# Weights of two k steps side by side: 1 MB transfers and a ring of six places for the experts of a one-layer recurrent decoder step

## The chip, the core and the metric

The kernel runs on one core of one Trainium2 chip. The engines named here are PE (matrix products), DVE and ACT (vector and scalar work), POOL and SP, which issue DMAs; SP here does nothing else. The metric is the device time of one execution in microseconds.

## What is computed

288 tokens (256 of a prompt, 8 sequences of 4 new ones) pass one layer: a norm, a mixer of two recurrent head groups, a second norm, then a mixture of 32 experts with four per token, an embedding term and a third norm. All is float32, and the width is 1024 throughout. Nearly all bytes are the experts' weights, three matrices of 4 MB for each of 32 experts:

```python
def _moe(x, w_router_l, b_router_l, wg, bg, wu, bu, wd, bd):
    logits = (xt @ w_router_l + b_router_l).astype(jnp.float32)
    top_v, top_i = lax.top_k(logits, TOP_K)
    gates = jax.nn.softmax(top_v, axis=-1)
    ...
        gate = xb @ wg[e] + bg[e]
        up = xb @ wu[e] + bu[e]
        gate = jnp.minimum(gate, SWIGLU_LIMIT)
        up = jnp.clip(up, -SWIGLU_LIMIT, SWIGLU_LIMIT)
        glu = gate * jax.nn.sigmoid(gate * SWIGLU_ALPHA)
        return ((up + 1.0) * glu) @ wd[e] + bd[e]
```

The layer's output adds to the normed x the experts' rows weighted by their gates, and `sigmoid(x @ w_ple_gate) * (p @ w_ple_proj)`.

## The kernel before

The kernel first runs the norm, the input projection (w_in), the recurrences, the output projection and the second norm, which writes the normed rows to `x1` (L1183 to L1191). PE transposes `x1` to `xT` (L420), and `xT` serves the router (L693) and the embedding gate (L737).

The experts are taken in pairs, 16 of them (`NPAIR`), each with a block of 64 rows per expert. In a pair there are three phases: **gate**, **up** and **down**. In each, `products` (L787) makes two bias products (L791) and then 8 k steps. A k step contracts 128 of the 1024 inputs for both experts q of the pair: the 64 gathered rows are the stationary side, the weights in the ring the moving one, in halves of 512 columns (L799). Beside the k steps PE does other work: in the gate phase it combines the pair before (`combine_unit`, L777, five units after k steps 1 to 5); in the up phase of pairs 0 to 13 it gathers rows for later pairs (`gather`, L763, after each odd k step, and a transpose of the gates at the end, L774), and in pairs 1 to 6 it makes one piece of the sample states (`sample_state`, L677).

Between up and down: DVE takes the up product in two halves (`up_half`, L1530), clamps it (L1536) and multiplies it with the gate part into `h_s` (L1538). PE transposes h (`h_transposes`, L810), four 128-column pieces for each half as soon as that half is there, ACT copies the result to `hTe`, and the down phase takes it as its stationary side. ACT copies the down product to `y_s` (L1118), which the next pair's combining units read.

**The ring** (L135) has 12 places of 128 x 1024 float32, 512 KB each. SP issues all loads in one fixed order (L296 to L306): first w_in in 2 KB rows, w_out, w_ple_gate and w_ple_proj (46 loads, `PRE`), then for each pair, matrix, k step and q one load of 4 KB rows, 48 per pair. Each waits until its place is free (`slot_free`, L275): it counts the products that last used the places (`slots_used`, or the phase's own count at the last k step). PE waits for each place by its own semaphore (L796). Input row kt * 128 + p lies in partition p, so a load reads one contiguous stretch of 512 KB.

After the pairs there may be further pairs for experts with more than 64 rows, by the same code in a loop that the data decides.

## Time and profile before

| | us |
|---|---|
| runs: median (lowest to highest) | 1408.85 (1405.63 to 1410.57) |
| the profiled execution | 1410.77 |
| its span in the profile | 1408.9 |
| PE busy | 1288.8 |
| weight loads on PE | 541.1 |
| DVE busy | 358.7 |
| ACT busy | 189.6 |
| SP's DMA queue | 430.79 MB in 121904 packets |

The profile is one execution. Its page has the busy time of each engine, then the span in 40 equal slices of 35.2 us with busy shares in tenths, the DMA engines' mean share and their rate. Views of the trace give the same for any stretch, or list instructions in order of time. A busy PE includes the ends of products that are modelled, so a phase is better measured from its first instruction to the next phase's first.

### The profile page before, as it was taken

What the parts mean: (1) busy time and instruction counts of PE and PEld (TensorE: products, weight loads), DVE (VectorE), ACT (ScalarE), POOL (GpSimd) and SP (SyncE); (2) the same over time, 40 slices, a digit from 0 to 9 for tenths busy, and PEclk for the clock granted to TensorE, in tenths of its full rate; (3) what the DMA queues carried; (4) which work ended last, traced back from release to release, by engine and by line L of the source; (5) the groups of instructions that cost most, each with busy time, mean ns of one, the idle gap of its engine ahead of it and who ended that gap; (6) DMA issues with size and microseconds to landing.
All of it is one profiled execution on the core that took longest, in us unless ns stands there. A gap on an engine that the chain in (4) does not pass through costs nothing.

```text
span 1408.9 us, 13053 instructions
## 1 busy us (share of the span) xinstructions
PE 1288.8 (91%) x5318; PEld 541.1 (38%) x5318; DVE 358.7 (25%) x528; ACT 189.6 (13%) x302; POOL 61.5 (4%) x64
## 2 busy tenths in 40 slices
PE   2899989779999999999999989999999999998984
PEld 2677678245443323233332323232333323232221
DVE  5665431334211212112121202111111211101124
ACT  3143221331110001010000101010100101010002
POOL 5000000420000000000010100000000000000000
PEclk9999975888999999999999989999999999999998
DMA  9723110121289999999999999999999999999993
GB/s 255 250 94 119 60 60 0 54 77 60 80 339 388 409 409 405 410 409 410 408 409 408 371 409 409 409 408 410 408 409 407 409 409 408 409 405 410 407 410 128
DMA packets 125614, 441.94 MB, mean 314 GB/s; under 512 B 14272, under 2 KB 14288, under 8 KB 125552
## 3 DMA queue, kind: packets, MB, share of 16 engines
q1 hardware_dynamic: 121904, 430.79, 78.4%
q0 software_dynamic: 3648, 10.27, 2.6%
q8 instruction: 45, 0.74, 0.2%
q14 instruction: 17, 0.14, 0.0%
HBM read 436.28 MB, written 4.73 MB: 313 GB/s over the span
## 4 chain that ended last, share of the span: by engine, by line
PE 76%; DMA 18%; ACT 2%; DVE 2%; issue 1%; SPq 1%; DVEq 0%
PE ps L799 38%; DMA ring<-in_w_gate 10%; PE ps L456 8%; PE ps L767 7%; PE ps L783 6%; DMA ring<-in_w_up 4%; PE ps L644 3%; PE ps L743 3%; DMA ring<-in_w_in 2%; DMA ring<-in_w_down 2%; PE ps L791 1%; PE ps L484 1%; ACT hTe L935 1%; PE ps L597 1%; PE ps L815 1%
## 5 line engine op out<-in xcount | busy, mean ns | idle before, releaser
L799 PE MATMUL ps<-ring,xTe 128*64 128x512 f32 x2048 | 482.6, 601 | 17.0 <-DMA ring<-in_w_up 8.4
L799 PEld LDWEIGHTS ps<-ring,xTe 128*64 128x64 f32 x2048 | 134.2, 136 | 316.6 <-issue 315.6
L799 PE MATMUL ps<-ring,hTe 128*64 128x512 f32 x1024 | 236.8, 612 | 16.8 <-DMA ring<-in_w_down 16.8
L1520 DVE TENSOR_TENSOR xs<-xs,ps 128x512 f32<-128x512 f32 (+1 forms) x96 | 65.7, 685 | 501.8 <-PE ps L783 501.6
L799 PEld LDWEIGHTS ps<-ring,hTe 128*64 128x64 f32 x1024 | 73.4, 140 | 173.0 <-issue 172.8
L456 PE MATMUL ps<-xT,ring 128*128 128x288 f32 x448 | 118.1, 422 | 6.3 <-DMA ring<-in_w_in 5.3
L767 PE MATMUL ps<-OH,x 128*128 128x256 f32 (+3 forms) x432 | 115.4, 389 | 0.0
L456 PEld LDWEIGHTS ps<-xT,ring 128*128 128x128 f32 x448 | 86.8, 197 | 32.7 <-DMA ring<-in_w_in 6.4
L767 PEld LDWEIGHTS ps<-OH,x 128*128 128x128 f32 (+1 forms) x432 | 67.3, 187 | 72.9 <-issue 66.5
L783 PE MATMUL ps<-y_s,GT 128*128 128x512 f32 (+1 forms) x192 | 88.2, 630 | 1.1 <-ACT y_s L935 1.1
L1536 DVE TENSOR_SCALAR h_s<-ps 128x512 f32<-128x512 f32 x32 | 22.0, 687 | 188.0 <-PE ps L799 188.0
L935 ACT ACTIVATE xTe<-ps 128x256 f32<-128x256 f32 (+1 forms) x60 | 23.9, 398 | 298.0 <-PE ps L767 298.0
L935 ACT ACTIVATE h_s<-g_s 128x1024 f32<-128x1024 f32 x16 | 16.9, 1057 | 324.6 <-DVE g_s L1526 324.6
L935 ACT ACTIVATE y_s<-ps 128x1024 f32<-128x1024 f32 x16 | 16.4, 1024 | 265.1 <-PE ps L799 265.1
L644 PE MATMUL ps<-ring,xT 128*128 128x512 f32 (+1 forms) x96 | 39.7, 635 | 8.8 <-DVE xT L1438 8.8
L783 PEld LDWEIGHTS ps<-y_s,GT 128*128 128x128 f32 (+1 forms) x192 | 21.4, 161 | 65.4 <-issue 61.3
L791 PE MATMUL ps<-bias,sel 96*128 96x512 bf16 x96 | 29.0, 384 | 13.3 <-ACT hTe L935 13.0
L743 PE MATMUL ps<-ring,xT 128*128 128x512 f32 (+1 forms) x96 | 38.5, 621 | 0.0
L935 ACT ACT_TABLE_LOAD x28 | 35.9, 1283 | 14.6 <-DVE mv L1181 12.2
L380 POOL TENSOR_TENSOR T<-V,cf 32x1024 f32<-32x1024 f32 x8 | 16.3, 2044 | 414.1 <-PE ps L686 348.7
L1526 DVE TENSOR_SCALAR g_s<-ps 128x1024 f32<-128x1024 f32 x16 | 19.6, 1225 | 33.9 <-PE ps L799 33.9
L644 PEld LDWEIGHTS ps<-ring,xT 128*128 128x128 f32 (+1 forms) x96 | 13.7, 174 | 32.5 <-issue 23.5
(304 smaller groups left out, 732.5 us busy)
## 6 DMA issues: line engine op xcount, KB each, us to landing
ring<-in_w_gate SPq DMA_DIRECT2D x256, 512.0 KB, 11.7
ring<-in_w_up SPq DMA_DIRECT2D x256, 512.0 KB, 11.4
ring<-in_w_down SPq DMA_DIRECT2D x256, 512.0 KB, 11.4
ring<-in_w_in SPq DMA_DIRECT2D x28, 512.0 KB, 5.7
ring<-in_w_out SPq DMA_DIRECT2D x8, 512.0 KB, 4.2
ring<-in_w_ple_gate SPq DMA_DIRECT2D x8, 512.0 KB, 3.7
S<-in_state_hgrn_S POOLq DMA_DIRECT2D x1, 2048.0 KB, 20.3
out<-S POOLq DMA_DIRECT2D x1, 2048.0 KB, 20.8
```

The lines of the kernel that those rows point to most:

```text
L380: nc.gpsimd.tensor_tensor(VB[n % len(VB)][0:NS, :].rearrange("p (b v) -> p b v", b=NSEQ), V[0:NS, 2, off:off + DV].unsqueeze(1).to_broadca ...
L456: last = mm(ps[:, bank, 0:NT], w, xT[:, k, :], start=k == 0, stop=k == KT - 1)
L644: last = mm(out_banks(i, half), HT[:, k, t0:t0 + r], w[:, half * 512:(half + 1) * 512], start=k == 0, stop=k == KT - 1)
L743: last = mm(ple_bank(i, half, bank), xT[:, k, t0:t0 + r], ring[:, n % RING, half * 512:(half + 1) * 512], start=k == 0, stop=k == KT - 1)
L767: last = mm(ps[:, bank, (k - k0) * w:(k - k0 + 1) * w], x1[0:r, i, k * P:(k + 1) * P], OH[0:r, i, c0:c0 + w], start=i == 0, stop=i == 2)
L783: last = mm(ps[lo:lo + r, CB_BANKS[n], :], gt[:, t0:t0 + r], y_s[:, half * 512:(half + 1) * 512], start=True, stop=True)
L791: mm(ps[:, bank0 + half, :], sel_p[:, :, :].rearrange("p q s -> p (q s)"), bias3[:, w, half * 512:(half + 1) * 512], start=True, stop=False)
L799: last = mm(ps[64 * q:64 * q + 64, bank0 + half, :], lhs(k, q), ring[:, s, half * 512:(half + 1) * 512], start=False, stop=k == KT - 1)
L935: return nc.scalar.activation(out, in_, func, **kw)
L1520: last = tt(x, x, ps[lo:lo + r, CB_BANKS[n], :], ALU.add)
L1526: ts(g_s[:, :], ps[:, 0:2, :].rearrange("p b n -> p (b n)"), LIMIT, None, ALU.min).then_inc(S["gl_ok"], 1)
L1536: ts(h_s[:, c], ps[:, 2 + half, :], LIMIT, -LIMIT, ALU.min, ALU.max).then_inc(S["u_ok"], 1)
```

## The change

Two things are regrouped. **Which input row lies in which partition**: not kt * 128 + p but p * 8 + kt, so that a partition owns eight consecutive input rows of a weight, and two consecutive k steps are 8 KB side by side in memory. **How the ring is used** by the experts: six places of 1 MB (`NWIDE`), 24 loads per pair (`PER = 3 * KT`), each with k steps 2 kw and 2 kw + 1 for one expert. A load's 128 rows then lie 32 KB apart. w_in, w_out and the embedding's weights keep loads of 512 KB; w_ple_gate and w_router only take the new row order.

Since contraction index k step kt, partition p now means input 8 p + kt, the other side of each product has to be in that order too. This is done where x1 and h are written, by DVE: `x1` and h get their columns reordered through `by_row`. h goes to `y_s` instead of `h_s`, each half of it fills 64 columns of each of the eight pieces, and so both halves have to be there before the first transpose. The transposes' own code stays.

```diff
-PER = 6 * KT
+NWIDE, PRE_WIDE = RING // 2, PRE // 2
+PER = 3 * KT
...
-    w_pg = a["w_ple_gate"][0].rearrange("(kt p) n -> kt p n", p=P)
+    w_pg = a["w_ple_gate"][0].rearrange("(p kt) n -> kt p n", p=P)
...
-    w_ex = [a[n].rearrange("l e (kt p) n -> (l e) kt p n", p=P) for n in ("w_gate", "w_up", "w_down")]
+    w_ex = [a[n].rearrange("l e (p kw k2) n -> (l e) kw p (k2 n)", p=P, k2=2) for n in ("w_gate", "w_up", "w_down")]
...
+        def wide(d):
+
+            return ring[:, 2 * (d % NWIDE):2 * (d % NWIDE) + 2, :]
...
+        def by_row(t):
+
+            return t.rearrange("r (k p) -> r p k", k=KT)
...
+            def wide_free(d, j=None):
+
+
+                if d - NWIDE < PRE_WIDE:
+                    return sp.wait_ge(S["slots_used"], 2 * (d - NWIDE) + 2)
+                p, t = divmod(d - NWIDE - PRE_WIDE, PER)
+                w, n = divmod(t, KT)
+                if n >= KT - 2:
+                    sem, count, per = S[("gate_mm", "up_mm", "y_mm")[w]], 4 * (p + 1), 4
                 else:
+                    sem, count, per = S["slots_used"], PRE + p * USED_PER + w * (KT - 2) + n + 1, USED_PER
+                sp.wait_ge(sem, count if j is None else j * per + count)
...
             for p in range(NPAIR):
-                for w in range(3):
-                    for k in range(KT):
-                        for q in range(2):
-                            ring_load(w_ex[w][2 * p + q, k], False)
+                for t, (w, k, q) in enumerate((w, k, q) for w in range(3) for k in range(KT // 2) for q in range(2)):
+                    d = PRE_WIDE + p * PER + t
+                    wide_free(d)
+                    sp.dma_start(wide(d).rearrange("p k n -> p (k n)"), w_ex[w][2 * p + q, k]
+                                 ).then_inc(slot_full[2 * (d % NWIDE)], 16)
...
                 for k in range(KT):
-                    slots = [(PRE + first + 2 * k + q) % RING for q in range(2)]
-                    for q, s in enumerate(slots):
-                        pe.wait_ge(slot_full[s], p * (16 * PER // RING) + 16 * ((PRE + first + 2 * k + q) // RING + 1))
+                    tiles = [first + 2 * (k // 2) + q for q in range(2)]
+                    if k % 2 == 0:
+                        for t in tiles:
+                            pe.wait_ge(slot_full[2 * ((PRE_WIDE + t) % NWIDE)], p * (16 * PER // NWIDE) + wide_full(t))
...
                             if k == KT - 1:
                                 last.then_inc(done, 1)
-                            elif half == 1:
+                            elif half == 1 and k % 2 == 1:
                                 last.then_inc(S["slots_used"], 1)
...
-                pe.wait_ge(S["h_ok"], p * 2 + (half + 1))
+                pe.wait_ge(S["h_ok"], p * 2 + 2)
...
-                    last = nc.tensor.transpose(ps[:, bank, j * P:(j + 1) * P], h_s[:, c:c + P], ident)
+                    last = nc.tensor.transpose(ps[:, bank, j * P:(j + 1) * P], y_s[:, c:c + P], ident)
...
-                out = x1[0:r, i, :] if 4 <= n < 7 else x
-                stt(out, x, mv[0:r, i, 3:4], ln_b[0:r, :], ALU.mult, ALU.add).then_inc(S["x_norm"], 1)
+                if 4 <= n < 7:
+                    last = stt(by_row(x1[0:r, i, :]), x.rearrange("r (p k) -> r p k", k=KT), mv[0:r, i, 3:4],
+                               ln_b[0:r, :].rearrange("r (p k) -> r p k", k=KT), ALU.mult, ALU.add)
...
-                    stt(h_s[:, c], h_s[:, c], 1.0, g_s[:, c], ALU.add, ALU.mult).then_inc(S["h_ok"], 1)
+                    stt(by_row(y_s[:, :])[:, 64 * half:64 * half + 64, :], h_s[:, c].rearrange("r (p k) -> r p k", k=KT), 1.0,
+                        g_s[:, c].rearrange("r (p k) -> r p k", k=KT), ALU.add, ALU.mult).then_inc(S["h_ok"], 1)
...
-                step(ts(xs[0:r, i, :], x1[0:r, i, :], ALPHA, None, ALU.mult))
+                step(ts(xs[0:r, i, :].rearrange("r (p k) -> r p k", k=KT), by_row(x1[0:r, i, :]), ALPHA, None, ALU.mult))
```

The queue of SP's loads over the gate and up phases of one pair, before; a row is one or several issues of a form, with the semaphore that frees the place (`y_mm` and `gate_mm` count the last k step of a phase):

```order
L293 DMA ring<-in_w_gate 128x1024 [waits slots_used] x10
L293 DMA ring<-in_w_gate 128x1024 [waits y_mm] x2
L293 DMA ring<-in_w_gate 128x1024 [waits slots_used] x4
L293 DMA ring<-in_w_up 128x1024 [waits slots_used] x10
L293 DMA ring<-in_w_up 128x1024 [waits gate_mm] x2
L293 DMA ring<-in_w_up 128x1024 [waits slots_used] x4
```

And with the change:

```order
L320 DMA ring<-in_w_gate 128x2048 [waits slots_used] x4
L320 DMA ring<-in_w_gate 128x2048 [waits y_mm] x2
L320 DMA ring<-in_w_gate 128x2048 [waits slots_used] x2
L320 DMA ring<-in_w_up 128x2048 [waits slots_used] x4
L320 DMA ring<-in_w_up 128x2048 [waits gate_mm] x2
L320 DMA ring<-in_w_up 128x2048 [waits slots_used] x2
```

There are half as many issues, each of 2048 columns, in the same order of matrices.

PE between the up and the down phase of pair 0, before (`cf` holds the identity for the transposes, `slot_full` a place's semaphore):

```order
L815 MATMUL ps<-cf,h_s 128x128 [waits h_ok]
L815 MATMUL ps<-cf,h_s 128x128 x3
L815 MATMUL ps<-cf,h_s 128x128 [waits h_ok]
L815 MATMUL ps<-cf,h_s 128x128 x3
L791 MATMUL ps<-bias_112,sel_113 128x512 [waits hTe_ok,GT_ok]
L791 MATMUL ps<-bias_112,sel_113 128x512
L799 MATMUL ps<-ring,hTe 64x512 [waits slot_full7,slot_full6]
L799 MATMUL ps<-ring,hTe 64x512 x3
L799 MATMUL ps<-ring,hTe 64x512 [waits slot_full9,slot_full8]
```

And with the change:

```order
L831 MATMUL ps<-cf,y_s 128x128 [waits h_ok]
L831 MATMUL ps<-cf,y_s 128x128 x3
L831 MATMUL ps<-cf,y_s 128x128 [waits h_ok]
L831 MATMUL ps<-cf,y_s 128x128 x3
L806 MATMUL ps<-bias_112,sel_113 128x512 [waits hTe_ok,GT_ok]
L806 MATMUL ps<-bias_112,sel_113 128x512
L815 MATMUL ps<-ring,hTe 64x512 [waits slot_full8,slot_full6]
L815 MATMUL ps<-ring,hTe 64x512 x7
L815 MATMUL ps<-ring,hTe 64x512 [waits slot_full0,slot_full10]
```

No instruction changes places. A pair of places is now waited for once for eight products instead of four, and both waits for `h_ok` ask for the second half.

## Rows read from the trace of the kernel before

**Rows 1.** The page: the DMA engines' rate in 40 slices.

```profile
GB/s 255 250 94 119 60 60 0 54 77 60 80 339 388 409 409 405 410 409 410 408 409 408 371 409 409 409 408 410 408 409 407 409 409 408 409 405 410 407 410 128
```

**Rows 2.** A window: length, busy PE, PEld, DVE, ACT, POOL, PE's clock, DMA share, GB/s.

```profile
600.00:800.00 200.00, 196.07 (x812) 65.69 (x809) 38.60 (x51) 16.11 (x29) 13.85 (x13) 1.00 1.03 408
```

**Rows 3.** The page's chain that ended last, by engine.

```profile
PE 76%; DMA 18%; ACT 2%; DVE 2%; issue 1%; SPq 1%; DVEq 0%
```

**Rows 4.** Timeline of PE: first products of pairs 0, 1, 2, 6, 7, 14, 15.

```profile
384.29 0.59 PE L791 MATMUL ps<-bias,sel 96*128 96x512 bf16 x2 [0.35 <-PE ps L757]
...
447.31 0.61 PE L791 MATMUL ps<-bias,sel 96*128 96x512 bf16 x2
...
508.24 0.61 PE L791 MATMUL ps<-bias,sel 96*128 96x512 bf16 x2
...
511.47 1.94 PE L799 MATMUL ps<-ring,xTe 128*64 128x512 f32 x8 [0.62 <-DMA ring<-in_w_gate]
...
755.22 0.60 PE L791 MATMUL ps<-bias,sel 96*128 96x512 bf16 x2
...
830.98 0.60 PE L791 MATMUL ps<-bias,sel 96*128 96x512 bf16 x2
...
1263.48 0.60 PE L791 MATMUL ps<-bias,sel 96*128 96x512 bf16 x2
...
1324.85 0.61 PE L791 MATMUL ps<-bias,sel 96*128 96x512 bf16 x2
```

**Rows 5.** Timeline of PE inside pairs 3 and 4.

```profile
617.84 13.95 PE L799 MATMUL ps<-ring,hTe 128*64 128x512 f32 x64
...
636.40 1.13 PE L783 MATMUL ps<-y_s,GT 128*128 128x512 f32 x2
...
665.91 1.98 PE L686 MATMUL ps<-T,AB 32*128 32x512 f32 x4
...
677.18 1.09 PE L815 MATMUL ps<-cf,h_s 128*128 128x128 f32 x8
```

**Rows 6.** PE's waits in pairs 7 to 13: total us, times, longest.

```profile
PE ps L799 <- DMA ring<-in_w_down: 7.8, 14, 0.6
PE ps L799 <- DMA ring<-in_w_gate: 4.3, 7, 0.6
```

**Rows 7.** The page: packets of SP's queue, and issues with median us to landing.

```profile
q1 hardware_dynamic: 121904, 430.79, 78.4%
...
ring<-in_w_ple_gate SPq DMA_DIRECT2D x8, 512.0 KB, 3.7
```

**Rows 8.** A window in which w_in is loaded.

```profile
44.00:48.00 4.00, 4.00 (x18) 3.16 (x17) 3.86 (x5) 0.41 (x1) 0.00 (x0) 1.00 1.05 388
```

**Rows 9.** Timeline of DVE, the end of pair 4's up phase.

```profile
676.36 0.69 DVE L1538 SCALAR_TENSOR_TENSOR h_s<-h_s,g_s 128x512 f32<-128x512 f32 x1
```

**Rows 10.** DVE by line and form: busy us, mean ns of one, idle before.

```profile
L1299 DVE TENSOR_TENSOR T<-KB,T 128x576 f32<-128x576 f32 x5 | 3.8, 753 | 3.3 <-PE ps L500 3.3
...
L1190 DVE SCALAR_TENSOR_TENSOR x<-xs,mv,ln_b 128x1024 f32<-128x1024 f32 x2 | 2.6, 1284 | 2.7 <-ACT mv L935 2.7
...
L1483 DVE TENSOR_REDUCE pick<-oneh 128x32 f32<-128x128 f32 x2 | 0.7, 372 | 0.1
...
L1481 DVE TENSOR_TENSOR oneh<-cf,top_f 128x128 f32<-128x128 f32 x2 | 0.6, 292 | 0.1
```

**Rows 11.** Timeline of PE, between up and down in pair 14.

```profile
1305.23 0.66 PE L815 MATMUL ps<-cf,h_s 128*128 128x128 f32 x4 [0.73 <-DVE h_s L1538]
```

**Rows 12.** Two links of the chain of waits after the second norm.

```profile
308.69 1.29 DVE x L1190
...
320.62 0.63 PE ps L430 x4
```

**Rows 13.** Timeline of DVE after the second norm, and ahead of the experts.

```profile
318.51 1.27 DVE L1190 SCALAR_TENSOR_TENSOR x<-xs,mv,ln_b 32x1024 f32<-32x1024 f32 x1 [0.64 <-ACT mv L935]
...
377.05 0.69 DVE L1546 TENSOR_TENSOR ple<-ple,ps 128x512 f32<-128x512 f32 x1 [21.41 <-PE ps L757]
```

More of the change, by code:

```diff
@@ L223, in trunk_step, with wide_full @@
         ps = ctx.enter_context(nc.psum_tensor("ps", [P, 8, 512], F32))
+        def wide(d):
+            return ring[:, 2 * (d % NWIDE):2 * (d % NWIDE) + 2, :]
+        def wide_full(t):
+            s = (PRE_WIDE + t) % NWIDE
+            return 16 * (len(range(2 * s, PRE, RING)) + len(range(s, PRE_WIDE + t + 1, NWIDE)) - len(range(s, PRE_WIDE, NWIDE)))
+        def by_row(t):
+            return t.rearrange("r (k p) -> r p k", k=KT)
         ident = cf[:, CF_IDENT:CF_IDENT + P]
@@ L302, in _ @@
             for p in range(NPAIR):
[L303 to L306 removed]
+                for t, (w, k, q) in enumerate((w, k, q) for w in range(3) for k in range(KT // 2) for q in range(2)):
[3 more added lines that the diff above has]
+                                 ).then_inc(slot_full[2 * (d % NWIDE)], 16)
             def extra_weights(j, e):
[L310 to L313 removed]
+                for t, (w, k, q) in enumerate((w, k, q) for w in range(3) for k in range(KT // 2) for q in range(2)):
+                    d = PRE_WIDE + NPAIR * PER + t
+                    wide_free(d, j)
+                    sp.dma_start(wide(d).rearrange("p k n -> p (k n)"),
                                  w_ex[w][bass.ds(e[q], 1), k, :, :].rearrange("e p n -> p (e n)")
[L315 removed]
+                                 ).then_inc(slot_full[2 * (d % NWIDE)], 16)
             sp.wait_ge(S["pos_ok"], 1)
@@ L793, in products @@
                 for k in range(KT):
-                    slots = [(PRE + first + 2 * k + q) % RING for q in range(2)]
-                    for q, s in enumerate(slots):
-                        pe.wait_ge(slot_full[s], p * (16 * PER // RING) + 16 * ((PRE + first + 2 * k + q) // RING + 1))
+                    tiles = [first + 2 * (k // 2) + q for q in range(2)]
+                    if k % 2 == 0:
+                        for t in tiles:
+                            pe.wait_ge(slot_full[2 * ((PRE_WIDE + t) % NWIDE)], p * (16 * PER // NWIDE) + wide_full(t))
                     for half in range(2):
-                        for q, s in enumerate(slots):
+                        for q, t in enumerate(tiles):
                             last = mm(ps[64 * q:64 * q + 64, bank0 + half, :], lhs(k, q),
-                                      ring[:, s, half * 512:(half + 1) * 512], start=False, stop=k == KT - 1)
+                                      wide(PRE_WIDE + t)[:, k % 2, half * 512:(half + 1) * 512], start=False, stop=k == KT - 1)
                             if k == KT - 1:
                                 last.then_inc(done, 1)
-                            elif half == 1:
+                            elif half == 1 and k % 2 == 1:
                                 last.then_inc(S["slots_used"], 1)
@@ L888, in _ @@
                 products(p, 0, 0, lhs, 0, sel[p % 2], lambda k: beside_gate(p, k), S["gate_mm"])
-                products(p, 2 * KT, 2, lhs, 1, sel[p % 2], lambda k: beside_up(p, k), S["up_mm"])
+                products(p, KT, 2, lhs, 1, sel[p % 2], lambda k: beside_up(p, k), S["up_mm"])
                 for half in range(2):
@@ L894, in _ @@
                 pe.wait_ge(S["hTe_ok"], 2 * p + 2)
-                products(p, 4 * KT, 4, lambda k, q: hTe[:, k, 64 * q:64 * q + 64], 2, sel[p % 2],
+                products(p, 2 * KT, 4, lambda k, q: hTe[:, k, 64 * q:64 * q + 64], 2, sel[p % 2],
                          nothing, S["y_mm"])
@@ L916, in _ @@
                         products(p, 0, 0, x_cols(xTe[0], 0), 0, sel[0], nothing, S["gate_mm"])
-                        products(p, 2 * KT, 2, x_cols(xTe[0], 0), 1, sel[0], nothing, S["up_mm"])
+                        products(p, KT, 2, x_cols(xTe[0], 0), 1, sel[0], nothing, S["up_mm"])
                         for half in range(2):
@@ L920, in _ @@
                         pe.wait_ge(S["hTe_ok"], j * 2 + (2 * NPAIR + 2))
-                        products(p, 4 * KT, 4, lambda k, q: hTe[:, k, 64 * q:64 * q + 64], 2, sel[0], nothing, S["y_mm"])
+                        products(p, 2 * KT, 4, lambda k, q: hTe[:, k, 64 * q:64 * q + 64], 2, sel[0], nothing, S["y_mm"])
                         pe.wait_ge(S["GT_ok"], j + (NPAIR + 1))
```

21 lines of the change are left out of this document (5 added, 16 removed).

## The prediction, made before the changed kernel ran

> **What bounds the kernel now.** I read the slices first. From slice 14 to slice 39 the rate stands at 405 to 410 GB/s with one dip [rows 1]: this is the expert stage, which moves 16 pairs x 24 MB = 403 MB. A window in it shows a DMA share of 1.03 and PE busy 196 of 200 us at full clock [rows 2]. So both are near their end at once, and the chain (PE 76%, DMA 18% [rows 3]) can't tell which gives way. For that I cut the stage into pairs of experts, by the first bias product of each gate phase [rows 4]. Numbering the pairs 0 to 15: pair 1 takes 508.24 - 447.31 = 60.9 us, with no wait for a DMA; pairs 1 to 5 take 61.6 on average; pair 6 takes 75.8 (the sample states are written out then); pairs 7 to 13 take (1263.48 - 830.98) / 7 = 61.8; pair 14 takes 61.4. The DMA's need for 24 MB at 408 GB/s is 61.7. PE's own need is 60.9 where it also makes a sample state (pairs 1 to 6), and 2.0 less, 58.9, in pairs 7 to 13, since the state's products cost 1.98 [rows 5]. There it waits for weights in short pieces, most in down and gate phases [rows 6]. So **pairs 1 to 6 are bound by PE and DMA almost alike, pairs 7 to 15 by the DMA**. Pair 0 takes 63 us of PE's work.
>
> **Part 1: the size of a piece of a transfer.** The DMA engines show 121,904 packets on SP's queue [rows 7]. Counting rows of the loads and outputs in the code gives 108,736, plus 16 per issue for 823 issues = 13,168: exactly that sum. So each row in a partition is one packet (the constants' rows of 4,384 bytes too), and I take an 8 KB row to be one. What is a packet's fixed cost? w_in comes in 2 KB rows and ran at 388 GB/s with a full share [rows 8]; the experts' 4 KB rows run at 408 to 409 [rows 2]. Per engine and 32 KB: 32,768 B / (388/16) = 1351 ns, and 1282 ns at 409. The 8 packets fewer save 69 ns, 8.7 ns each. Going to 8 KB saves 4 more, and half a semaphore packet: 1282 - 39 = 1243 ns, or 421 GB/s. **A 1 MB transfer then takes 2.49 us, a pair 59.8 us**, 2.0 less than the 61.8 of pairs 7 to 13. Bounds: no gain at all (2.57 us), or nothing left of the cost (about 1.5% more still).
> The Trainium skill ("DMA: Bandwidth & Descriptors", Why small descriptors are slow) gives about 3 cycles per packet beside one per 32 bytes. By it 128 + 3 becomes 256 + 3, a gain of 1.1% and not 3%, and the sum below would end near +13 us rather than +6. The row at 388 speaks for the larger cost.
>
> **Part 2: the ring.** Six places of 1 MB hold what twelve of 512 KB held, but a place comes free only after two k steps, and PE needs two places whole to start. What is the price? Where PE is slower than the DMA (the up phase, with gathers), the ring is full at the start of a down phase, D. PE does 8 k steps in 13.95 us [rows 5], so it frees two places at D + 4.0, 7.5, 10.9 and 14.4. A transfer of 512 KB on an idle queue landed 3.7 us after its issue [rows 7], 2.4 more than its 1.28 on the engines (the experts' own landing times are time in the queue). So the down phase's fourth piece (k 6 and 7) lands at 4.0 + 2.4 + 5.0 = 11.4, where PE wants it at 10.9: wait 0.4. The next two land 5.0 apart, at 16.4 and 21.3. PE wants them at 14.4 + 0.4 + 0.5 = 15.4 (wait 1.0) and at 16.4 + 3.5 + 1.2 = 21.0, with a combining unit (1.13 and the switch) between [rows 5] (wait 0.3). Then units of 1.2 after each k step make PE slower than the DMA again. **Total 1.7 us per pair.** Before, with a full ring and single places, the same sum gives no wait: pair 1 has none.
>
> **Part 3: h is written scattered.** Each half of h now goes to y_s with neighbours 512 bytes apart, and both halves are needed before the first transpose. Where gathers run, the second half's product ends at 676.36 + 0.69 = 677.05 [rows 9] and the transposes start at 677.18, when PE gets there [rows 5]: the lost overlap costs nothing there. But any lengthening d of the two products shows, less 0.13. ACT's copies and PE's down phase stand behind it. In pairs 14 and 15 PE already waits for h [rows 11], but there the DMA is the bound and catches it. No write of this kind is in the trace. Nearest row: a reduction that reads elements 128 bytes apart takes 372 ns for 128 elements, where a product of 128 takes 292 [rows 10]: 80 more, so 0.34 us per 512 written elements. d = 0.68, less 0.13 = 0.55 per pair. Bounds: 0, and a doubling of what an element costs, i.e. the same operation's 1,024-element form less its 512 one (1.28 - 0.69 = 0.59 each) [rows 10], 1.05 per pair. I take 0.55, the only row with far-apart elements.
> The Trainium skill ("SBUF — State Buffer", Door 1) says that each access crossing to a new 16-byte line pays a penalty. It speaks against this change, and gives no figure; by it the case of no cost is out.
>
> **The sum**, stage by stage, for d' = 0.55:
> Pairs 1 to 6: 60.9 + 1.7 + d' against 61.6: +1.6 each, +9.6 (pair 6 keeps its stall).
> Pairs 7 to 13: 58.9 + 1.7 + d' = 61.2 (more than the DMA's 59.8) against 61.8: -0.6 each, -4.0.
> Pair 14: the DMA's 59.8 against 61.4: -1.6. Pair 15: -1.6, but after the last byte two k steps remain and not one, +1.7: 0.
> Pair 0: 0.4 + d' = +1.0.
> Expert stage: +5.0.
> Ahead of it: x1 is written scattered three times after the second norm. The first is in the chain (1.29 us [rows 12]), the third ends at 318.51 + 1.27 = 319.78 [rows 13], 0.8 before its transposes start. With 0.67 more on each, the third ends at 321.8 and PE starts about 1.2 later than 320.62; 0 or 2.7 at the bounds. The scaling of x1 into xs lies in an idle stretch of DVE (21.4 us before L1546 [rows 13]), and its longer time is hidden. w_ple_gate and w_router are loaded long before use.
> Total +6.2: the profiled execution goes from 1410.8 (span 1408.9) to 1417.0. The median of the runs shown, 1408.85, is 1.9 below the profiled one, so **1415.1**.
>
> **Rivals.**
> A. Scattered writes are free. For: products that read and write runs of 1 to 16 elements with gaps as long stay at 753 ns for 576 [rows 10], like packed ones. Against: the gaps there are short. Sum: 5.0 - 14 x 0.55 = -2.7, nothing ahead: 1406.1.
> B. An element costs double. Sum: 5.0 + 14 x 0.50 + 2.7 = +14.7: 1423.6. It decides from d' = 1.1 us or so, where pairs 7 to 13 too become no shorter than they were (58.9 + 1.7 + d' = 61.8).
> C. 8 KB rows bring no rate (cut in two, or the pitch of 32 KB between a partition's rows costs what the length gives). Transfer 2.57: waits 2.2, pairs 1 to 6 +2.1 each, 7 to 13 none, 14 none, 15 +1.7, pair 0 +1.2, front +1.2: +17, 1425.5. This is also the case in which the change doesn't do what it says.
> D. The refill waits don't arise, since transfers land sooner after a place is free than I have it. Then pairs 7 to 13 fall to the DMA's 59.8 (-14), pairs 1 to 6 keep still (-0.6), 14 and 15 -1.5, pair 0 and front +1.7: -14.4, 1394.5. Against: pair 2 already waits in its gate phase although pair 1 had none to wait for [rows 4], so lead times under load are not shorter than I take them.
>
> **Chances.** Forecast 0.34, A 0.27, B 0.19, C 0.10, D 0.10. A measurement can tell about 0.3%, 4.2 us, from no change. Each case has some 4 us to either side from the lead time of a transfer. Faster: D 0.10, A 0.13, forecast 0.04 = 0.27. Same: A 0.12, forecast 0.10, B 0.01 = 0.23. Slower: C 0.10, B 0.18, forecast 0.20, A 0.02 = 0.50. The range takes in A, B, most of C and the nearer half of D: 1397 to 1426. The forecast's own range is 1410 to 1421.
>
> **What would show it.** Packets on SP's queue down by 49,152 + 6,144, and 421 GB/s in windows without idle DMA. DVE's h product at 1.03 us (0.69 for A, 1.28 for B). Pairs 1 to 6 at 63.2, pairs 7 to 13 at 61.2, pair 14 at 59.8. DMA share below 1 in the up phases, as the ring is full. PE waiting for gate weights in pieces of about 1 us at k 0, and at k 2, never between. I am wrong if the DMA share stays at 1.03 through pairs 7 to 13, or if the rate is not near 420.

## The result, and the profile after

| | before | after | forecast |
|---|---|---|---|
| median of the runs | 1408.99 us (6 runs, 1405.63 to 1410.57) | 1429.27 us (6 runs, 1428.57 to 1437.48) | 1415.1 |
| profiled execution: time, span | 1410.8, 1408.9 | 1429.0, 1427.2 | 1417.0 |
| pairs 1 to 5, mean | 61.6 | 63.8 | 63.2 |
| pairs 6 and 7 | 75.8, 61.9 | 70.9, 66.3 | 77.4, 61.2 |
| pairs 8 to 13, mean | 61.8 | 61.8 | 61.2 |
| pair 14; pair 15 and the end | 61.4; 84.1 | 63.3; 87.7 | 59.8; 84.1 |

The change made the kernel slower: ratio 1.0157, 95% interval 1.0132 to 1.0182. I had forecast slower, but by 6 us and not by 20; the time lies 3 us outside the range. (Periods of pairs are cut as in [rows 4]: from one gate phase's bias product to the next.)

The page of the changed kernel, its DMA rate in 40 slices and SP's queue, which answer to [rows 1, 7]:

```profile
GB/s 255 247 90 118 59 59 0 62 68 59 109 344 390 418 379 378 422 378 422 360 421 379 410 400 408 379 397 423 400 422 397 411 407 397 422 397 422 381 399 94
...
q1 hardware_dynamic: 66608, 430.77, 75.0%
```

The packets fell by 121,904 - 66,608 = 55,296, exactly the 49,152 + 6,144 foreseen, and where the queue is never empty the rate is 422 GB/s. But the slices no longer stand at one level: those at 422 alternate with ones at 360 to 400. Windows of the changed kernel (length, busy PE, PEld, DVE, ACT, POOL, PE's clock, DMA share, GB/s), first the one of [rows 2], then pair 9: its gate phase, and the turn from up to down:

```profile
600.00:800.00 200.00, 190.79 (x786) 64.93 (x782) 38.12 (x48) 16.25 (x29) 7.51 (x4) 0.99 0.96 395
971.00:975.00 4.00, 3.73 (x16) 1.13 (x14) 0.69 (x1) 0.00 (x0) 0.00 (x0) 1.00 1.01 424
...
1015.00:1018.00 3.00, 3.00 (x16) 1.01 (x14) 0.00 (x0) 0.00 (x0) 0.00 (x0) 1.00 0.85 352
1018.00:1021.00 3.00, 3.00 (x16) 1.01 (x14) 0.00 (x0) 0.00 (x0) 0.00 (x0) 1.00 0.71 229
1021.00:1024.00 3.00, 3.00 (x16) 1.00 (x14) 0.00 (x0) 0.00 (x0) 0.00 (x0) 1.00 1.01 418
```

A faster DMA moved less: 395 GB/s over 600:800, where it was 408. It pauses for a while in each pair, while PE is busy. The timeline of PE at that pause (start, us, engine, line, operation, records, idle before it and its releaser) tells why:

```profile
1005.43 3.65 PE L815 MATMUL ps<-ring,xTe 128*64 128x512 f32 x16
1009.01 1.75 PE L782 MATMUL ps<-OH,x 128*128 128x256 f32 x6
1010.70 0.61 PE L789 MATMUL ps<-cf,GW 128*128 128x128 f32 x3
1011.79 1.09 PE L831 MATMUL ps<-cf,y_s 128*128 128x128 f32 x8 [0.48 <-DVE y_s L1558]
1013.71 0.59 PE L806 MATMUL ps<-bias,sel 96*128 96x512 bf16 x2 [0.83 <-ACT hTe L951]
1014.23 10.52 PE L815 MATMUL ps<-ring,hTe 128*64 128x512 f32 x48
1025.93 3.65 PE L815 MATMUL ps<-ring,hTe 128*64 128x512 f32 x16 [1.18 <-DMA ring<-in_w_down]
...
1030.90 3.65 PE L815 MATMUL ps<-ring,xTe 128*64 128x512 f32 x16 [0.78 <-DMA ring<-in_w_gate]
```

Up's last k step ends at 1009.0 and gives back two places. The next two come back when down's second k step is over, at 14.2 + 3.6 = 1017.9. For 8.9 us nothing is freed; the ring fills up, and the DMA stands. PE pays for it at the end of the down phase (1.18) and at the next gate (0.78). Before, a place was half as large and came back after one k step, and the share stayed at 1.01 to 1.03 there.

### The profile page after: what moved, and what is told of

Read it like the earlier page. It is cut to its first block, busy times and chain, and to the rows that moved or that the text cites. A ratio compares the mean times of both kernels' runs of the same rounds, so it can differ in the third digit from the quotient of the medians.

```text
span 1427.2 us, 12477 instructions
## 1 busy us (share of the span) xinstructions
PE 1285.9 (90%) x5318; PEld 551.2 (39%) x5318; DVE 369.8 (26%) x528; ACT 189.5 (13%) x302; POOL 61.1 (4%) x64
## 3 DMA queue, kind: packets, MB, share of 16 engines
q1 hardware_dynamic: 66608, 430.77, 75.0%
## 4 chain that ended last, share of the span: by engine, by line
PE 69%; DMA 21%; DVE 6%; ACT 2%; issue 1%; SPq 1%; DVEq 0%
PE ps L815 36%; DMA ring<-in_w_gate 11%; PE ps L471 8%; PE ps L782 6%; DMA ring<-in_w_up 6%; PE ps L798 4%; PE ps L758 3%; PE ps L659 3%; DMA ring<-in_w_in 2%; DVE y_s L1558 2%; DMA ring<-in_w_down 2%; DVE h_s L1556 1%; PE ps L499 1%; PE ps L806 1%; ACT hTe L951 1%
## 5 line engine op out<-in xcount | busy, mean ns | idle before, releaser
L815 PE MATMUL ps<-ring,xTe 128*64 128x512 f32 x2048 | 477.5, 601 | 29.8 <-DMA ring<-in_w_gate 19.4
L815 PEld LDWEIGHTS ps<-ring,xTe 128*64 128x64 f32 x2048 | 140.6, 137 | 320.1 <-issue 319.8
L815 PE MATMUL ps<-ring,hTe 128*64 128x512 f32 x1024 | 234.2, 610 | 14.4 <-DMA ring<-in_w_down 14.4
L798 PEld LDWEIGHTS ps<-y_s,GT 128*128 128x128 f32 (+1 forms) x192 | 21.4, 161 | 65.4 <-issue 61.3
L1558 DVE SCALAR_TENSOR_TENSOR y_s<-h_s,g_s 128x512 f32<-128x512 f32 x32 | 33.4, 1043 | 1.1
L831 PE MATMUL ps<-cf,y_s 128*128 128x128 f32 x128 | 19.2, 298 | 12.0 <-DVE y_s L1558 12.0
## 6 DMA issues: line engine op xcount, KB each, us to landing
S<-in_state_hgrn_S POOLq DMA_DIRECT2D x1, 2048.0 KB, 20.3
```

The source lines that it names most:

```text
L798: last = mm(ps[lo:lo + r, CB_BANKS[n], :], gt[:, t0:t0 + r], y_s[:, half * 512:(half + 1) * 512], start=True, stop=True)
L815: last = mm(ps[64 * q:64 * q + 64, bank0 + half, :], lhs(k, q), wide(PRE_WIDE + t)[:, k % 2, half * 512:(half + 1) * 512], start=False, st ...
L831: last = nc.tensor.transpose(ps[:, bank, j * P:(j + 1) * P], y_s[:, c:c + P], ident)
L1558: stt(by_row(y_s[:, :])[:, 64 * half:64 * half + 64, :], h_s[:, c].rearrange("r (p k) -> r p k", k=KT), 1.0, g_s[:, c].rearrange("r (p k) ...
```

## The experiments

All ratios are to the kernel before, which ran beside them at 1408.75 to 1409.44 us. Four parts can be told apart: the row order with scattered writes, the size of the places, the 8 KB rows, and what PE does.

### The parts alone

**e_fine**: the kernel before (twelve places of 512 KB, 4 KB rows) with the row order and the scattered writes.

```diff
-    w_ex = [a[n].rearrange("l e (kt p) n -> (l e) kt p n", p=P) ...
+    w_ex = [a[n].rearrange("l e (p kt) n -> (l e) kt p n", p=P) ...
```

> The row order of the change alone (partition p owns input rows 8p to 8p+7, h and x1 written scattered, both halves of h awaited), but loads of one k step, 4 KB rows, 512 KB, in the old ring of twelve places. If the coarse ring is what costs (my theory now: places of 1 MB come free late and are refilled late), this kernel stands near the one before: rate 408 to 409, pairs 1 to 6 at 61.8, pairs 7 to 13 at 61.8, plus 0.9 ahead of the experts and 1 to 2 at pairs 14 and 15: 1411 to 1414. If the new row order costs (rows 32 KB apart, the scattered writes), it stands near the changed kernel: 1425 to 1430, and the first of the two shows as a rate below 405.

Measured 1420.24 us (1.0088, 1.0065 to 1.011), at 407 GB/s over 905:1263, for 408 before: the pitch of 32 KB between rows costs the DMA nothing that shows, but the row order costs 11 us with a fine ring, more than I gave it.

**e_wide4k**: six places of 1 MB and transfers of 1 MB, but in the old order, so in 4 KB rows, with plain writes.

```diff
-    w_ex = [a[n].rearrange("l e (p kw k2) n -> (l e) kw p (k2 n)", p=P, k2=2) ...
+    w_ex = [a[n].rearrange("l e (kw k2 p) n -> (l e) kw p k2 n", p=P, k2=2) ...
```

> The coarse ring alone: six places of 1 MB, transfers of 1 MB, but the old row order, so each partition gets two rows of 4 KB, and h and x1 are written plainly and awaited by halves as before. Coarse ring theory: rate 409, pairs 1 to 6 at 60.9 + 2.5 = 63.4, pairs 7 to 13 at 61.7 to 62, the last two about 1.5 longer than before: 1420 to 1426. Row order theory: as before, 1407 to 1411.

Measured 1429.88 us (1.0157, 1.0138 to 1.0175). **The coarse ring alone costs 21 us**, as much as the whole change. A window in pairs 8 to 13, of this kernel, then the same one of the kernel before, shows PE busy 4.6 us less in the same time:

```profile
905.00:1263.00 358.00, 337.57 (x1409) 116.16 (x1405) 60.66 (x84) 28.78 (x50) 0.00 (x0) 1.00 1.02 405
```

```profile
905.00:1263.00 358.00, 342.13 (x1430) 114.98 (x1428) 59.90 (x83) 29.66 (x53) 0.00 (x0) 1.00 1.03 408
```

In pairs 1 to 5 a pair takes 64.4 us for 61.6; that is 14 of the 19 us between the two spans. Three things are coarse here at once: the places, the transfers that fill them, and the 2 MB that come back together. No run changes one of them alone.

**e_plain**: the changed kernel with h, x1 and the scaled x1 written plainly. Both halves of h are still awaited together. The weights' rows then meet other elements of x1 and h, so the experts' and the embedding gate's part of the result is not the reference's.

```diff
-                    stt(by_row(y_s[:, :])[:, 64 * half:64 * half + 64, :], h_s[:, c].rearrange("r (p k) -> r p k", k=KT), 1.0, ...
+                    stt(y_s[:, c], h_s[:, c], 1.0, g_s[:, c], ALU.add, ALU.mult)
```

> The changed kernel with h, x1 and the scaling of x1 written and read plainly (the contraction then pairs the wrong rows, so the experts' part of the output is not the reference's; the work is the same). Expected, if the scattered writes cost what DVE's 1.04 us and PE's waits of 0.48 show: 0.48 less in pairs 0 to 13, 1 to 2 less in 14 and 15, 0.9 less ahead: 1417 to 1420. If DVE's time were covered: no change from 1429. If it carries the whole loss: 1409.

Measured 1415.32 us (1.0047, 1.003 to 1.0063). So the writes cost 14.0 of the change's 20.3 us. And beside e_wide4k, which has the same ring, **the 8 KB rows give back 14.6 us**, and a little more, since e_wide4k may start on the first half of h alone: in each of pairs 14 and 15 it waits 1.4 us for h, and e_plain 2.06.

**e_pestride**: the changed kernel with h written plainly, and PE's transposes reading every eighth column of it; x1 as in the change.

```diff
-                    last = nc.tensor.transpose(ps[:, bank, j * P:(j + 1) * P], y_s[:, c:c + P], ident)
+                    last = nc.tensor.transpose(ps[:, bank, j * P:(j + 1) * P], h_s[:, 4 * half + j:D:KT], ident)
```

> The changed kernel, but h is written plainly and PE's transposes read every eighth column of it instead. If a strided read is free on PE: as e_plain plus 0.9 for x1, 1418 to 1421. If PE reads strided elements at a lower pace (transposes at 2 times 0.14 us each per pair), up to 1.1 us per pair more: 1433.

Measured 1419.14 us (1.0073, 1.0054 to 1.0093): the scattered h is 10.1 of the 14.0 us, x1 the other 3.8. The runs' intervals leave some 3 to 4 us to either side of each such difference. The step is not quite free for PE either: in pairs 0 to 13 the eight transposes take 1.16 us for 1.09. Their weight loads, in e_pestride and then in the changed kernel (window 390:1290):

```profile
L830 PEld LDWEIGHTS ps<-cf,h_s 128*128 128x128 f32 x112 | 13.6, 194 | 0.6
```

```profile
L831 PEld LDWEIGHTS ps<-cf,y_s 128*128 128x128 f32 x112 | 12.0, 141 | 8.3 <-DVE y_s L1558 8.3
```

### The ring

**e_before8** and **e_after8**: one line, `RING = 12` to `RING = 8`, in the kernel before and in the changed one: 4 MB instead of 6.

> The kernel before with eight 512 KB places instead of twelve (4 MB). 3 MB are left to run ahead of the step in use. Theory of the coarse ring: between the change's 4 MB (1429 less its other parts) and four wide places' 2 MB: 1425 to 1460, and well under e_after8. Rival, depth hardly matters: 1409 to 1415.

> The changed kernel with four 1 MB places instead of six (4 MB), nothing else. Theory of the coarse ring: only 2 MB, some 5 us of transfer, can run ahead of the place in use, less than the gathers and the hand-over of h hold the TensorE and about the time from a freed place to its landed refill (3.1 us) plus the other place; each pair loses 4 to 8 us: 1480 to 1560. Rival, depth hardly matters and the writes do: 1429 to 1440.

Measured 1459.17 us (1.0357, 1.0325 to 1.0388) and 1645.78 us (1.1658, 1.1606 to 1.1709), the second 86 us over the upper end of what I expected. With 4 MB in fine places the kernel loses 50 us, and in coarse ones 217 over the change. I read depth and grain as one thing, how much of the ring is not in use. PE holds one 1 MB step of it before, and 2 MB after, so 5, 4, 3 and 2 MB are left in the kernel before, e_wide4k, e_before8 and e_after8, which take 1409, 1430, 1459 and 1646 us (the last also has the scattered writes and 8 KB rows). PE's waits in e_after8 (total us, times, longest):

```profile
PE ps L815 <- DMA ring<-in_w_down: 73.8, 19, 6.3
PE ps L815 <- DMA ring<-in_w_gate: 63.1, 40, 3.5
PE ps L815 <- DMA ring<-in_w_up: 54.0, 37, 3.8
```

**e_qfirst** and **e_qfirst_pe**: can coarse places come back one by one? The block of expert q=0 on both k steps goes ahead of that of q=1; the second kernel also writes all plainly and has PE read x1 and h with a step.

```diff
+                    if k < KT - 2:
+                        steps = [(kk, half, k % 2) for kk in (k - k % 2, k - k % 2 + 1) for half in range(2)]
...
+                    for kk, half, q in steps:
+                        last = mm(ps[64 * q:64 * q + 64, bank0 + half, :], lhs(kk, q), ...
```

> The changed kernel, with the four matmuls of expert q=0 on both k steps of a 1 MB place issued ahead of the four of q=1 (k steps 0 to 5; 6 and 7 as they are). The same matmuls, as many between two gathers or combine units; only each expert's tile is waited for when its own block comes, and its place is given back a block (about 0.85 us) earlier. Theory of the coarse ring (two places of 1 MB given back together leave 4 of 6 MB to run ahead; the old kernel's places left 5): a ring whose places come back one by one leaves 5 MB again, so 1412 to 1419 us against the change's 1429.3, the pair's waits on DMA at gate k2 and up k2/k4/k6 gone. Rival, the scattered writes or the matmul side are what costs: 1426 to 1430, the waits as they were.

> The same, with h, x1 and the scaled x1 written plainly and every reordering left to TensorE, which reads x1 and h with a step of 8 columns (as it did for h without a visible cost). Theory of the coarse ring, with the row order's DVE cost (1.0 us per h, 1.3 us per x1 tile) taken away: the 8 KB rate is left alone, so 1396 to 1405 us, under the old kernel's 1409. Rival, the row order costs through something other than the writes: 1412 or more.

Measured 1642.1 us (1.1658, 1.1639 to 1.1678) and 1667.1 us (1.1825, 1.1805 to 1.1845), so this said nothing about the ring, but much about PE. The timeline of e_qfirst, where x8 is four matmuls:

```profile
1114.00 3.65 PE L818 MATMUL ps<-ring,xTe 128*64 128x512 f32 x8
```

Four matmuls take 3.65 us, the time of eight in the changed kernel (x16 above). The two experts' products go to rows 0 to 63 and 64 to 127 of the result, and two of them run at once only while q alternates. The Trainium skill says in "TensorEngine Tiling (Array Packing)", Key Properties, that tiles operate independently and can run in parallel; this trace agrees.

### PE beside the DMA

**e_half_before** and **e_half_after**: each expert product on 256 columns instead of 512, in both kernels; the other columns of the products hold the bias only.

```diff
-                            last = mm(ps[64 * q:64 * q + 64, bank0 + half, :], lhs(k, q), ...
+                            last = mm(ps[64 * q:64 * q + 64, bank0 + half, 0:256], lhs(k, q), ...
```

> The kernel before with its expert products on half the columns (each matmul 256 instead of 512; the other half of h and y holds only the bias), all transfers as they are. It leaves TensorE some 38 us of a 61 us pair, so the pairs run at the rate of the weights alone: 61.4 us (24 MB at 409 GB/s). Theory of two bounds (TensorE is busy 60.5 us in pairs 1 to 6 and 58.5 in 7 to 13, and must wait 1.3 us more for the hand-over of h, so it has as little room as the DMA): only the gaps of pairs 1 to 6 and the end of pair 15 go: 1380 to 1400 us. Rival, TensorE had room and the DMA alone is the bound: 1390 to 1405, which tells little by itself; the two runs are read together.

> The changed kernel with the same halved products. Theory of two bounds: with TensorE out of the way the 8 KB rows show their whole worth, 59.8 us per pair instead of 61.4: 20 to 25 us under e_half_before, the pairs at 59.8 +- 0.4, since neither the coarse ring nor the DVE's writes can hold back a TensorE with 20 us to spare. Rival, the coarse ring or the row order holds back the DMA queue whatever TensorE does: within 8 us of e_half_before.

Measured 1404.13 us (0.9964, 0.9953 to 0.9974) and 1393.3 us (0.988, 0.9862 to 0.9898): 11 us between them, half of the 20 to 25. (e_half_before lies 4 us over my theory's 1380 to 1400, within its rival's range.) Windows of e_half_after tell where the rest is:

```profile
536.00:540.00 4.00, 4.00 (x8) 1.26 (x10) 0.45 (x1) 0.00 (x0) 0.41 (x1) 0.50 1.01 422
540.00:544.00 4.00, 4.00 (x14) 2.08 (x10) 0.77 (x1) 0.00 (x0) 1.48 (x1) 0.50 0.78 279
...
905.00:1263.00 358.00, 265.74 (x1461) 139.43 (x1460) 63.84 (x85) 30.68 (x54) 0.00 (x0) 0.89 1.01 420
```

From 905 on it does keep to 420 GB/s. The first two windows are of pair 2's up phase: PE, which had waited 2.49 and 1.76 us for weights, runs at a granted clock of 0.50 (1.2 of 2.4 GHz), is slow just where it has most to do, and the DMA's share falls to 0.78. I take it that the coarse ring is full there. e_half_before's PE waits too (its clock is 0.87 on average in pairs 1 to 6, for 0.84), but with its fine ring the share is 1.03 over these pairs and 1.02 over 905:1263.

**e_thin_before** and **e_thin_after**: the gathers for later pairs make one matmul of 32 rows instead of three (the prompt's rows are left out of them).

```diff
                     for i, (_, r) in enumerate(TILES):
+                        if w == 128 or i == 2:
...
-                                  OH[0:r, i, c0:c0 + w], start=i == 0, stop=i == 2)
+                                      OH[0:r, i, c0:c0 + w], start=w > 128 or i == 0, stop=i == 2)
```

> The kernel before with the gathers for later pairs cut from three matmuls to the one of 32 rows (the rows of the two prompt tiles are left out of xTe), all signals and transfers as they are. It takes 1.1 us from each of four gathers, 4.5 us of TensorE time from each pair of 0 to 13, with its clock kept high. Theory of two bounds: the DMA's 61.4 us per pair stays, so 1400 to 1408 us. Rival, TensorE alone is the bound of this kernel: 4 us less per pair, 1350 to 1370.

> The changed kernel with the same thin gathers. Theory of two bounds and a coarse ring: without those 4.5 us TensorE's path is 57 us in pairs 1 to 6 and 55 in 7 to 13, under the DMA's 59.8, and the time between two freed pairs of places shrinks too: 1390 to 1402 us, 27 to 40 less than the change and under e_thin_before by 3 to 15, the pairs at 59.8 to 61. Rival, the landing time of a refill holds it whatever TensorE does: 1412 or more, over e_thin_before.

Measured 1406.66 us (0.9984, 0.9973 to 0.9995), as expected: the kernel before keeps the DMA at 408 GB/s and has PE at its heels. And 1439.45 us (1.0204, 1.0179 to 1.023): **with some 60 us less to do for PE (14 pairs, four gathers each at 0.69 us and not 1.75) the changed kernel is 10 us slower**. The rival's "1412 or more" holds, but neither theory had it slower than the change. Its windows at the turn from up to down in pair 9:

```profile
1020.00:1022.00 2.00, 2.00 (x6) 0.55 (x8) 0.00 (x0) 0.00 (x0) 0.00 (x0) 0.50 1.01 422
1022.00:1024.00 2.00, 2.00 (x10) 0.62 (x8) 0.00 (x0) 0.00 (x0) 0.00 (x0) 0.69 1.01 422
1024.00:1026.00 2.00, 2.00 (x12) 0.58 (x10) 0.00 (x0) 0.00 (x0) 0.00 (x0) 1.00 0.17 66
1026.00:1028.00 2.00, 2.00 (x12) 0.68 (x10) 0.00 (x0) 0.00 (x0) 0.00 (x0) 1.00 0.63 131
```

Three things come together. The gather that stood between up's last k step and the transposes had covered the DVE's two products of h; with it thin, PE waits for h (26.5 us in all instead of 12.0). PE's waits for weights grow more, from 44 to 73 us. After such a wait the clock is 0.50, so down's first k steps take longer. And the stretch without a freed place grows with both, so the DMA stands longer (share 0.17, then 0.63). No run splits the 10 us among them.

**e_mg_before**, **e_mg_after**: the four gathers moved from up's k steps 1, 3, 5, 7 to down's 0, 2, 4, 6, to even out the phases. **e_mg2_before**, **e_mg2_after**: only two of them moved, to down's k steps 1 and 3, behind a freed place.

```diff
+            def beside_down(p, k):
+                if p < GATHERS and k % 2 == 0:          # e_mg2: k in (1, 3)
...
+                    gather(xTe[g % 2], 4 * (p % 2) + n, 1, 6 + n % 2, 0, 256)
```

> The kernel before with its four gathers for the next pairs moved from behind up's k steps 1, 3, 5, 7 to behind down's 0, 2, 4, 6 (and ACT's and DVE's copies behind those of h), nothing else. Gate, up and down then take TensorE 20, 19 and 21 us instead of 20, 26 and 14, while the weights of each take the DMA 20.5. Theory: the ring of 5 free MB already carries the uneven phases over, so it gives little: 1402 to 1412. Rival, uneven phases cost the kernel before too: 1395 or less.

> The changed kernel with the same move. Theory of the coarse ring (its 4 free MB run full during the long up phase, the DMA pauses, and TensorE starves at the start of down and of gate): with even phases the ring never runs full, and most of the change's 20 us come back: 1403 to 1415. Rival, it is the landing time of a 1 MB refill and not the uneven phases: 1420 to 1430.

> The kernel before with only the third and fourth gather moved: up keeps two, behind its k steps 1 and 3, and down takes two, behind its k steps 1 and 3. Gate, up and down take TensorE 20, 23 and 18 us. Theory: as e_mg_before, little to gain with fine places: 1403 to 1413 us. Rival, even phases help by themselves: under 1400.

> The changed kernel with the same move. In e_mg_after the gathers stood behind even k steps, between the two k steps of one place, and put 1.75 us more ahead of the first place that down frees; the ring then stood full for some 8 us of each down phase. Here they stand behind odd k steps, after a place was freed. Theory of the gap between freed places (what costs is the stretch in which TensorE frees nothing and the six places run full): the gap at up to down is that of the change and the long up phase is shorter: 1410 to 1425. Rival, any work moved into down costs the changed kernel as in e_mg_after: 1450 to 1495.

Measured 1413.87 us (1.0025, 1.0014 to 1.0036) and 1415.06 us (1.0042, 1.0028 to 1.0057) for the old kernel, 1495.78 us (1.0622, 1.0599 to 1.0646) and 1447.26 us (1.0271, 1.0248 to 1.0293) for the changed one. The old kernel's are 2 us over what I expected; of the changed one's, the first is 66 us over even its rival's range and the second 3 us under its rival's. Evening out the phases gained nothing; what is moved into down makes the kernel slower. A gather between down's first two k steps adds 1.75 us to it, and those taken from up's end had covered the wait for h (the line below, for 12.0 us in the changed kernel). Windows of e_mg_after, one in gate and two in down, and PE's wait for h in e_mg2_after:

```profile
1018.00:1022.00 4.00, 4.00 (x18) 1.02 (x14) 0.95 (x2) 0.00 (x0) 0.00 (x0) 1.00 0.99 342
...
1054.00:1058.00 4.00, 4.00 (x16) 1.53 (x14) 0.00 (x0) 0.38 (x1) 0.00 (x0) 0.83 0.38 154
1058.00:1062.00 4.00, 4.00 (x19) 1.42 (x15) 0.00 (x0) 0.00 (x0) 0.00 (x0) 1.00 0.45 139
```

```profile
PE ps L831 <- DVE y_s L1562: 35.0, 16, 2.6
```

One thing stays open: in pair 9's gate phase (the first window) e_mg_after moves only 342 GB/s at a share of 0.99, and no run settles why.

### Fine places where they are wanted

**e_mix**: gate's and up's weights as in the change, down's in 512 KB transfers of 4 KB rows and the old order, two to a place (one for each expert), given back after one k step. h is plain and its halves are waited for apart; x1 is plain and read by PE with a step of 8. **e_mix2**: the same, with x1 written scattered by the DVE.

```diff
+                    if w == 2:
+                        for e in range(2):
+                            sp.dma_start(wide(d)[:, e, :], w_dn[2 * p + e, 2 * k + q]).then_inc(slot_full[2 * (d % NWIDE)], 16)
```

> Gate's and up's weights as in the change (8 KB rows, 1 MB places given back two by two), down's weights as before it (4 KB rows in the old order, k step by k step in half places, each place given back after one k step). h is written plainly and its halves waited for apart, x1 is written plainly and read with a step of 8 columns by TensorE. The DMA needs 16 x 2.49 + 16 x 1.28 = 60.3 us per pair. Theory of the stretch without a freed place (the six places run full between up's last k step and down's second, so what matters is that down's first place comes back after 1.8 us and not 3.65): the DMA no longer stops at the start of down, 1398 to 1409 us. Rival, the coarse places cost wherever they are: e_plain, which differs from this in down alone, took 1415, so 1412 or more.

> e_mix with x1 written by the DVE in row order as in the change, instead of read with a step of 8 columns as a stationary operand: e_mix showed that such a weight load takes 330 ns instead of 189 (a gather 2.10 us instead of 1.75, the ones of pair 0 7.5 instead of some 4.4, the start of pair 0 7 us later). Down's places fine, gate's and up's coarse, h plain. Theory that only those loads spoiled e_mix, and that a fine first place in down is what the change lacks: 1444 less 20 at the front and in pair 0 and less 4 x 0.35 x 14 = 20 in the gathers: 1402 to 1409 us. Rival, coarse places cost wherever they are: 1413 to 1420, no better than e_plain.

e_mix took 1444.45 us (1.0249, 1.0225 to 1.0273). Its weight loads of x1 tell why; PEld of e_mix, then of the changed kernel:

```profile
L796 PEld LDWEIGHTS ps<-OH,x 128*128 128x128 f32 x288 | 74.1, 330 | 49.9 <-issue 48.8
```

```profile
L782 PEld LDWEIGHTS ps<-OH,x 128*128 128x128 f32 x288 | 46.3, 189 | 52.4 <-issue 47.9
```

330 ns instead of 189; in the transposes of e_pestride the same step cost less, 194 ns for 141. With 1444 us e_mix lies outside the 1398 to 1409 of its theory. e_mix2 took **1411.0 us** (1.0015, 1.0004 to 1.0026), 2 us over what I expected and below the rival's 1413, 4 under e_plain although it still has x1's 3.8. Its pairs 8 to 13 take 60.5 to 61.3 (mean 60.8, for 61.8 before), and its window answers to the two above:

```profile
905.00:1263.00 358.00, 343.85 (x1450) 117.47 (x1448) 61.31 (x85) 29.66 (x53) 0.00 (x0) 1.00 1.01 414
```

In each of these pairs the down phase takes 14.4 us, with no wait for weights, and all of PE's waits for them are at gate, where the places are still coarse. Against the kernel before it gains nothing: pairs 1 to 5 are at 62.9 for 61.6, and x1 adds 2 at the front. No version here that does the whole work beats the kernel before.

## Why the prediction was wrong, step by step

**Part 1 was right.** 8 KB rows are one packet, 421 GB/s was foreseen and 420 to 426 measured, and e_plain against e_wide4k shows 14.6 us for it. In the prediction the same is C against A plus the writes: C gave 1425.5 with the rate missing and the writes in, the forecast 1415.1, so 10.4. The 4.2 us more are hardly clear of the runs' intervals, and nothing shows where they come from.

**Part 2 is the step that failed**: "Total 1.7 us per pair", added to PE's own 60.9 and 58.9, with the DMA's 59.8 as the time of pair 14. But for 0.4 in pair 0 and 1.7 in pair 15 that is the whole of the ring in my sum. Take the writes out: rival A's sum gives 1406.1, and e_plain took 1415.3. In the profiled executions 8.0 of the 9.2 us missing show (e_plain's periods less those of before, against A's terms): pairs 1 to 5 +7.9 and not +5.2; pairs 6 and 7 -2.4 and not -0.1; **pairs 8 to 13 -0.7 and not -6.7**; pair 14 +0.4 and not -1.6; the rest within some 1 each.

Three things in it were too small. The first is PE's own time, and over pairs 1 to 13 it weighs about as much as the second, the waits. I took pair 1 for it, the shortest pair: a pair less its waits for weights takes 61.3 in pairs 1 to 5 of e_plain (61.3 to 61.5 in pairs 2 to 5 of the kernel before) and not 60.9, and 59.3 in pairs 8 to 13 (59.9 in the kernel before) and not 58.9. The waits are 1.8 us per pair in pairs 1 to 5, as foreseen, but 2.4 in pairs 8 to 13, 1.6 in some and 3.7 in pair 13. PE's waits for weights in e_plain's pairs 8 to 13 (window 897.86:1267.82):

```profile
PE ps L815 <- DMA ring<-in_w_down: 6.9, 6, 2.1
PE ps L815 <- DMA ring<-in_w_gate: 6.3, 12, 0.8
...
PE ps L815 <- DMA ring<-in_w_up: 1.2, 3, 0.6
```

The third is pair 14, which I let take the DMA's 59.8: it takes 61.8 in e_plain, since the DMA itself stands there (windows below).

The single waits were near: in pair 9 of the changed kernel 1.18 at down's k 6 (I had 0.4; counted from down's bias product, the weights landed at 12.2 and not 11.4, and PE wanted them at 11.0 and not 10.9), then 0.78 and 0.27 at gate for 1.0 and 0.3. I had worked out one cycle from a full ring and let every pair be like it. The DMA, though, loses what it stands: the share in 905:1263 is 0.99 at 410 GB/s where a full queue gives 422 at 1.01. That what it loses in one pair PE is made to wait for in a later one is my reading of this; no run tests it. e_wide4k, which is case C without the writes (1425.5 less 7 x 0.55 and 1.2), should have come at about 1420 by my working, and took 1430.

**Part 3 had the right cost of one write** (1.03 us foreseen, below), and in all the writes took 14.0 us and not 9.0 (1415.1 less A's 1406.1), just clear of the runs' intervals. DVE of the changed kernel, by line and form (busy us, mean ns), beside [rows 9, 10]:

```profile
L1558 DVE SCALAR_TENSOR_TENSOR y_s<-h_s,g_s 128x512 f32<-128x512 f32 x32 | 33.4, 1043 | 1.1
...
L1206 DVE SCALAR_TENSOR_TENSOR x<-xs,mv,ln_b 128x1024 f32<-128x1024 f32 x2 | 3.9, 1972 | 2.7 <-ACT mv L951 2.7
...
L1609 DVE TENSOR_SCALAR xs<-x 128x1024 f32<-128x1024 f32 x2 | 2.6, 1296 | 0.0
```

The row with a step of 128 bytes was a good guide: 0.69 to 1.04 us per 512 elements, 1.28 to 1.97 per 1024. For h I had 14 x 0.55 = 7.7, and it is 10.1; for x1 1.2, and it is 3.8, of which 2.0 show as PE's wait for x1 (7.4 us in all, and 5.4 in e_plain). The 0.55 itself was met: PE waits 0.48 us for h in pairs 0 to 13. What I dropped was pairs 14 and 15: "there the DMA is the bound and catches it". The timeline of pair 14, with the windows that follow it:

```profile
1319.84 1.97 PE L831 MATMUL ps<-cf,y_s 128*128 128x128 f32 x8 [2.65 <-DVE y_s L1558]
...
1322.49 1.04 PE L806 MATMUL ps<-bias,sel 96*128 96x512 bf16 x2 [0.69 <-ACT hTe L951]
```

```profile
1320.00:1324.00 4.00, 3.31 (x12) 1.83 (x14) 0.00 (x0) 1.19 (x2) 0.00 (x0) 0.50 1.01 422
1324.00:1328.00 4.00, 4.00 (x16) 1.19 (x14) 0.00 (x0) 0.00 (x0) 0.00 (x0) 0.71 0.63 260
1328.00:1332.00 4.00, 4.00 (x22) 1.33 (x20) 0.00 (x0) 0.00 (x0) 0.00 (x0) 1.00 0.61 205
```

No gather covers the products of h here. PE waits 2.65 us, comes back at half clock, and the transposes take 1.97 us for 1.09; meanwhile the DMA's share falls to 0.6. The bound that should have caught the wait stood still itself. But most of this is not the writes'. e_plain, with h written plainly, shows nearly the same in its pair 14:

```profile
1309.72 1.50 PE L831 MATMUL ps<-cf,y_s 128*128 128x128 f32 x8 [2.06 <-DVE y_s L1554]
```

```profile
1310.00:1314.00 4.00, 3.31 (x14) 1.46 (x14) 0.00 (x0) 1.19 (x2) 0.00 (x0) 0.53 1.02 424
1314.00:1318.00 4.00, 4.00 (x12) 0.99 (x12) 0.00 (x0) 0.00 (x0) 0.00 (x0) 0.61 0.73 301
1318.00:1322.00 4.00, 4.00 (x22) 1.39 (x20) 0.00 (x0) 0.00 (x0) 0.00 (x0) 1.00 0.58 197
```

In place of -1.6 and 0, pairs 14 and 15 became +1.9 and +3.6; in e_plain they are +0.4 and +0.5. Nor are the 4.6 us between all h's. In pair 15 of the changed kernel up's last two k steps take 5.35 us for 3.65, behind a wait of 2.53 for weights, and the granted clock of 1376:1380 is 0.69. e_pestride, where h is plain too, has the same in its pair 15, which takes 87.4, in an execution 6 us over that kernel's median; e_plain's pair 15 has not. The line of e_pestride:

```profile
1373.59 5.35 PE L815 MATMUL ps<-ring,xTe 128*64 128x512 f32 x16 [2.67 <-DMA ring<-in_w_up]
```

So where the 5 us lie that the writes took over my 9.0 stays open. Two slips changed nothing: 80 ns for 128 elements make 0.32 us for 512 and not 0.34, and what is left of the packets' cost at 8 KB is 39 of 1243 ns, 3% and not 1.5.

**Rivals.** A had the writes free: wrong, they are 14.0 us. C (1425.5) came nearest in time, but not by its cause: the rate was there. B (1423.6) was next, and an element did not cost double. D was wrong: the refill waits arose. The chance of 0.50 for slower was given for the right mechanisms at too small a size.

**Two tests of mine told less than I hoped.** e_half and e_thin were meant to take PE off the bound. In the changed kernel PE then waited more, came back at half clock after such waits, and they measured that too.

## What to carry to other kernels

Judge a ring between a DMA and an engine by the longest stretch in which the engine frees nothing: add the hand-over, the first steps up to the first freed place, and the start of a transfer, and compare it with the ring less what is in use. Longer rows gave 14.6 us here, and the coarse places that came with them took 21; ask for both prices. Take an engine's own time from the mean of its pairs less their waits, and not from the shortest pair. And work that looks like load in an engine's queue, like the gather behind up's last step, may be the cover of another engine's tail.
